# Low parts of twelve weight slabs computed by GpSimd instead of VectorE in a two-block transformer kernel

## The reference

```python
h = h + swa_sink_mixer(hn, ...)      # ends in: return o.reshape(B, S, ATTN_WIDTH) @ w_o + b_o
h = h + swiglu(rms_norm(h, ffn_norm[layer]), ffn_w_gu[layer], ffn_w_down[layer])
h = h + nsa_mixer(hn, ...)           # ends in: return o.reshape(B, S, ATTN_WIDTH) @ w_o
```

## Time and profile before

| what | us |
| --- | --- |
| median of 3 runs | 960.89 (960.56 to 962.05) |
| profiled execution, whole | 961.82 |
| its span, first to last instruction | 960.0 |
| PE busy | 938.5 (98%) |
| DVE busy | 736.5 (77%) |
| ACT busy | 545.1 (57%) |
| POOL busy | 102.3 (11%) |
| line 1777, 291 low parts on DVE | 353.7 |
| line 1218, 291 high parts on ACT | 295.9 |

### The profile page before, as it was taken

How to read it: one execution, slowest core, us unless ns; L and a number is a source line. 1 busy time by engine, 2 the same in 40 slices (tenths; PEclk the granted TensorE clock), 3 DMA queues, 4 the chain that set the end, 5 groups by cost and what they waited for, 6 DMA issues and landing times.

```text
span 960.0 us, 16452 instructions
## 1 busy us (share of the span) xinstructions
PE 938.5 (98%) x6364; PEld 842.7 (88%) x6364; DVE 736.5 (77%) x1531; ACT 545.1 (57%) x1061; POOL 102.3 (11%) x134
## 2 busy tenths in 40 slices
PE   7989999999999999999999999999999999999997
PEld 7989899988888889889888888899877988888887
DVE  6889855697777675966998888768898589888871
ACT  6667653566555465776644444558687564444452
POOL 3110002300000050003110101210000110100120
PEclk8999999999999999999999999999999999999999
DMA  8977235496454464316945645557311346445621
GB/s 284 239 193 218 88 133 176 152 259 227 158 214 175 175 220 143 121 46 198 272 159 214 220 160 191 203 173 258 113 46 45 136 173 219 177 148 201 220 88 44
DMA packets 25983, 165.12 MB, mean 172 GB/s; under 512 B 3320, under 2 KB 3704, under 8 KB 7472
## 3 DMA queue, kind: packets, MB, share of 16 engines
q1 hardware_dynamic: 23504, 156.09, 46.7%
q0 software_dynamic: 2400, 7.97, 4.4%
HBM read 161.03 MB, written 3.01 MB: 171 GB/s over the span
## 4 chain that ended last, share of the span: by engine, by line
PE 85%; DVE 5%; ACT 4%; DMA 4%; issue 1%; SPq 0%; POOL 0%; DVEq 0%
PE banks L591 22%; PE banks L911 13%; PE banks L594 11%; PE banks L915 8%; PE banks L565 4%; PE banks L569 4%; PE banks L573 4%; DMA scratch<-VR 3%; PE banks L614 3%; PE banks L616 2%; PE banks L618 2%; ACT PN L1462 1%; PE banks L840 1%; PE banks L576 1%; PE banks L577 1%
## 5 line engine op out<-in xcount | busy, mean ns | idle before, releaser
L1777 DVE TENSOR_TENSOR lo<-stage,hi 128x1024 fp32r<-128x1024 f32 x291 | 353.7, 1230 | 19.9 <-ACT hi L1218 18.2
L1218 ACT ACTIVATE hi<-stage 128x1024 fp32r<-128x1024 f32 x291 | 295.9, 1043 | 28.0 <-DMA stage<-in_stream 13.9
L591 PE MATMUL banks<-HT,hi 128*128 128x512 f32 x920 | 232.2, 394 | 0.0
L591 PEld LDWEIGHTS banks<-HT,hi 128*128 128x128 f32 x920 | 165.1, 188 | 33.7
L594 PEld LDWEIGHTS banks<-HT,lo 128*128 128x128 f32 x920 | 125.4, 189 | 9.7
L594 PE MATMUL banks<-HT,lo 128*128 128x256 f32 x920 | 128.0, 282 | 0.0
L2538 POOL TENSOR_TENSOR SQ<-SQ 128x256 f32<-128x256 f32 x40 | 43.4, 1091 | 422.9 <-ACT SQ L1236 421.9
L2276 DVE TENSOR_REDUCE U<-banks 128x256 f32<-128x512 f32 x73 | 50.3, 690 | 29.6 <-PE banks L594 29.2
L911 PE MATMUL banks<-HC,hi 128*128 128x512 f32 x196 | 70.5, 398 | 0.0
L565 PE MATMUL banks<-HT,hi 128*128 128x256 f32 (+3 forms) x348 | 56.3, 297 | 9.7 <-ACT HT L1228 4.9
L915 PE MATMUL banks<-HC,lo 128*128 128x256 f32 x224 | 63.0, 281 | 0.0
(11 more groups left out here) (348 smaller groups left out, 1785.8 us busy)
## 6 DMA issues: line engine op xcount, KB each, us to landing
stage<-in_stream SPq DMA_DIRECT2D x144, 1024.0 KB, 4.9
BT<-scratch POOLq DMA_DIRECT2D x8, 256.0 KB, 15.9
BT<-scratch POOLq DMA_DIRECT2D x4, 512.0 KB, 17.4
stage<-in_stream SPq DMA_DIRECT2D x3, 512.0 KB, 9.7
scratch<-VR POOLq DMA_DIRECT2D x2, 768.0 KB, 21.3
XT<-in_xt SPq DMA_DIRECT2D x4, 256.0 KB, 6.5
B<-scratch POOLq DMA_DIRECT2D x4, 256.0 KB, 6.4
out<-ROWS SPq DMA_DIRECT2D x4, 256.0 KB, 2.5
```

The source lines that it names most:

```text
L591: e.matmul(out[:, 0:512], hi[:, j % HI_SLOTS, 128 * k:128 * k + 128], HT[:, :, k, :], start=k == 0, stop=False)
L1218: e.activation(hi[:, j % HI_SLOTS, 0:w], stage[:, j // 2 % ST_PAIRS, j % 2, 0:w], ACT.Copy).then_inc(*up("hi", ("hi", j, 0)))
L1777: e.tensor_tensor(lo[x], stage[x], f32(hi[:, j % HI_SLOTS, 0:sched[j][2]]), ALU.subtract).then_inc(*up("lo", ("lo", j, 0)))
```

## The change

VectorE leaves out the low parts of slabs 2 to 7 of `swa_o` and of `nsa_o`, twelve in all. GpSimd does the same subtraction from the same operands, each after the high part of its slab, and counts up a semaphore of its own, `lo_pool`. In its list the first six stand behind the sum of squares of the swa layer, the other six behind the copies into `BC`. TensorE waits for the low part of a slab as before, by key. Nothing else changes.

```diff
+    "sums", "pool_step", "branch", "silu", "lo_pool",
...
+    pool_lows = {name: [slab[name, i] for i in range(2, 8)] for name in ("swa_o", "nsa_o")}
...
-        slabs = Splits(sched, lambda j: None, low_split)
+        others = set(pool_lows["swa_o"] + pool_lows["nsa_o"])
+        slabs = Splits(sched, lambda j: None, lambda j: None if j in others else low_split(j))
...
     def gpsimd(e):
         q = Queue(e)
 
+        def low_splits(name):
+
+            for j in pool_lows[name]:
+                q.wait_ge(*at("hi", j, 0))
+                e.tensor_tensor(lo[:, j // 2 % ST_PAIRS, j % 2], stage[:, j // 2 % ST_PAIRS, j % 2], f32(hi[:, j % HI_SLOTS]), ALU.subtract).then_inc(*up("lo_pool", ("lo", j, 0)))
...
         sum_squares("swa", both=True)
+        low_splits("swa_o")
         sum_squares("mlp2")
...
         e.tensor_copy(BC[:, :, 16:23], BT[:, :, 159:256:16]).then_inc(*up("pool_step", ("bc",)))
+        low_splits("nsa_o")
         sum_squares("mlp3")
```

More of the change, by code:

```diff
@@ L170 @@
     "lo", "low", "sums_dve", "x", "root_dve", "z", "top", "probabilities", "key_dve", "query_dve", "step",
-    "sums", "pool_step", "branch", "silu",
+    "sums", "pool_step", "branch", "silu", "lo_pool",
     "w0", "w1", "w2", "w3", "w4", "w5", "wone2", "wfirst0", "wfirst1", "x0", "x1", "x2", "x3", "columns", "masks",
```

## The result

| what | before | after |
| --- | --- | --- |
| median of 5 runs each, us | 962.05 (960.56 to 962.40) | 974.17 (972.24 to 975.21) |
| ratio after to before | | 1.0131 (95% interval 1.0115 to 1.0147) |
| profiled execution, whole | 961.8 | 974.2 |
| its span | 960.0 | 972.4 |

The change makes the kernel 12.1 us slower (by the interval of the ratio 11.1 to 14.1). The forecast was 972.3 us, with 962.0 to 979.5 as its range and 0.84 on slower. The total came out as forecast, but not by the terms of the forecast's sum: the blocked port cost less than forecast, and a clock that fell, which no step of the prediction had, made up for it.

What follows compares the result with a forecast made beforehand. TensorE was taken to bound both attentions, in the third waiting for a ring through ScalarE and VectorE. Port costs 8.9 + 2.5 = 11.4 us on 961.8 gave 973.2, less 0.9 for the median 972.3 us; range 962.0 to 979.5.

Steps and rivals of the forecast that it cites:

- third attention, port: Third attention: GpSimd's subtractions block VectorE's small two-SBUF lines in six steps, 2.4 + 5 x 1.3 = 8.9 us.
- second attention, port: Second attention: GpSimd's subtractions may hold up VectorE's tensor_scalars and so TensorE; taken at 2.5 us.
- relief of VectorE: Both attentions: removing 14.6 us of low parts from VectorE gains nothing, as they lie off the path TensorE waits for.
- the ring through ScalarE and VectorE: Third attention: a cycle of steps through both engines, 7.69 us from one line 1706 on, that sets TensorE's waits.
- Hold of 2.4 us: Both attentions: each 128x1024 GpSimd subtraction takes 2.4 us and excludes VectorE's two-SBUF instructions for its whole length.
- First slab 2.4: Third attention, first moved slab: GpSimd gets the port first and line 2496 waits, 2.4 us.
- Five slabs at 1.3 each: Third attention, other five moved slabs: VectorE's line 2496 goes first, then line 2451 comes 1.3 us late each time.
- Second attention 2.5 between 0 and 3.6: Second attention: 0 if tensor_scalars don't wait for the port, up to 3.6 us if they do; 2.5 taken.
- (1): Rival, both attentions: exclusion not felt, as GpSimd fits in a 1.07 us gap or 64-element instructions slip past; 960.7 us, chance 0.12.
- (2): Rival, both attentions: GpSimd wins the port each time, 6 x 2.4 + 3.6 = 18 us more, 978.9 us; chance 0.19.
- (3): Rival: the hold is shorter (1.22 to 2 us) or tensor_scalars don't wait; 963 to 969.8 us, chance 0.19.
- (4): Rival, both attentions: low parts are on TensorE's path and its waits go, 4.0 us less, 956.9 us; chance 0.04.

Runs made afterwards that it cites:

- e10: The change, with one ScalarE high part in step 5 of the second attention put behind the scale of the query tile: 972.11 us, ratio 1.0112.
- e3: The kernel before without the twelve low parts, computed by nobody; TensorE multiplies the high part again in their place: 960.67 us, ratio 0.9988.
- e5: The change, but GpSimd subtracts only the first 256 of 1024 columns of each slab and VectorE the rest, after it: 963.86 us, ratio 1.0033.
- e4: The change, but each GpSimd subtraction also waits until VectorE's small lines that need the port are over: 961.33 us, ratio 0.9999.
- e7: The change, but GpSimd copies each of the twelve slabs (one operand) instead of subtracting, so low parts are wrong: 961.41 us, ratio 1.0003.
- e9: e4 with one ScalarE high part in step 5 of the second attention put behind the scale of the query tile: 960.92 us, ratio 0.9985.
- e6: The change, but GpSimd subtracts only the first 512 of 1024 columns of each slab and VectorE the rest, after it: 965.62 us, ratio 1.0052.
- e1: The change with only the second attention's six low parts (swa_o) on GpSimd, those of nsa_o back on VectorE: 964.83 us, ratio 1.0030.

## Why the prediction was right, and which of its steps were not

The difference of 12.4 us between the profiled executions, in terms of the prediction's sum:

| term | forecast | measured | shown by |
| --- | --- | --- | --- |
| third attention, port | 8.9 | 7.1 | rings of e10 |
| second attention, port | 2.5 | 2.2 | the change's steps: 0.03 + 0.66 + 0.44 and 1.04 at ZR; no run forces it apart from the clock |
| relief of VectorE | 0 | 0.7 at best, not taken by the change | e3 |
| TensorE at half clock | not in the sum | 1.5 + 2.1 | second attention: 4.60 against 3.08 us for the same work; third: rings 4 and 5 against e10 |
| rest of the kernel | 0 | -0.5 | scatter ahead of the second attention |

- **What bounds the kernel.** Right: the ring through ScalarE and VectorE in the third attention. The ring table shows it, and e3 shows that a gain ahead of it is given back (0.2 us gained and lost again in the next step).
- **Relief costs and gives nothing.** Right in the third attention. In the second it gives 0.65 us at ZR (e3): the ZR path of VectorE and ScalarE does have a low part in it. It is small beside the rest.
- **Hold of 2.4 us.** Right: 2.34 to 2.39 us alone and 2.5 to 2.6 where it waits for line 2499 or 1853. This was extrapolated from 0.59 us for 256 elements behind the lock; four times that is 2.36. The Trainium skill (GPSIMD Engine Reference, "3. Performance versus the Vector engine") gave 2.4 as well; the trace agrees with its 2.6 cycles an element for two inputs: 0.73 us for 256 elements in e5 and 2.37 for 1024 make 2.1 ns an element, by the page's 1.2 GHz an estimate of 2.6 cycles.
- **First slab 2.4.** GpSimd goes first there, as forecast, but the instruction that it overtook, by 0.09 us, was the tensor_scalar of line 2493, ahead of line 2499, and it cost 2.1 us. The prediction had line 2496 (now 2499) wait there, and counted tensor_scalars in the second attention alone.
- **Five slabs at 1.3 each.** This is the term that was too large: 6.5 forecast, 5.0 in e10, where the clock stays up in these rings or costs nothing. In the change they are 0.7, 1.05, nothing, 1.1 and 1.05. The 0.7 is that of a step that also scales a query tile ahead of line 2454, by which the gap is 1.39 us and not 1.07; the prediction took one step as the model of all. VectorE wins the port, as taken, and line 2454 is late, as taken. But GpSimd had already started 0.1 us before line 2499 took the port, so its own start is not paid again behind the lock: from the end of line 2499 (715.37) to GpSimd's (717.61) are 2.24 us, and line 2454 at 716.42 is 1.05 us longer, since its own start is covered by the wait too (it ends 0.08 us after GpSimd). The fourth slab meets nothing in the change: behind the fall of the clock line 2454 comes only after GpSimd has ended (727.8 against 728.05), where in e10 it is blocked by 1.1.
- **Second attention 2.5 between 0 and 3.6.** The open question, whether tensor_scalars from SBUF to SBUF wait, is answered: the pair of line 2163 takes 1.90 us instead of 0.55. This is what the Trainium skill states (SBUF — State Buffer, "SBUF: two separate sides", with Advanced Engine Details and Errata, "VectorE Performance Modes"): the trace agrees. What the blocked pairs cost came out lower than the 3.6 us that the prediction worked out for this case: 2.2, and the 3.7 of the whole only with the clock. The path to TensorE was right too, over ZR, where the waits are seen.
- **The clock.** No step of the prediction asked what TensorE's idle time does to its clock. In the change it stands at half for 6.8 us in the third attention and 3.4 in the second, and 3.6 of the 12.4 us are lost to that. In the third attention this is a difference between two kernels that differ in the second attention only, so it is well supported; that the idle time causes the fall is a reading of the traces, not something an experiment forced. For it: each fall in the two attentions stands behind a wait of 1.5 us or more, and the kernels with the small losses, e3, e4 and e7 to e9, have 1.00 in both. Against idle time alone: behind waits of 3.0 and 2.8 us in the change and of 2.3 us in e10 the clock stayed up.
- **The rivals.** (1) is right that short holds are free: up to 1.14 us behind the end of line 2502 in e6 (2499 of the change), a little over the 1.07 that the prediction gave. The hold simply is 2.4, and its other reason, that a 64-element instruction slips past, is wrong (1.27 instead of 0.22). (2) happens for one slab of six, by the 0.1 us between the two starts. (3) is wrong on both counts. (4) is wrong: with no low parts at all the gain is 0.7 us, not 4.0.

So the total was right to 0.2% while 2.1 us of overestimate and 3.6 us of a missing term cancelled in part. The sign, the place and the mechanism stand; that the total came this close was luck.

What stays open: what decides whether the clock falls. With the same wait for ZR of 2.1 us it fell in e1, e5 and the change and not in e6, and e10's third attention was spared in its fourth ring while that of the change was not. As the executions of e6 differ by up to 3.6 us and in their mean clock, one profile of a kernel shows one case of several, and the 3.6 us of the clock hold for the profiled execution alone.

## What to carry to other kernels

An engine that has nothing to do is not a free engine: look at which of the neighbour's instructions need the port that it takes, and whether one of them, however small, lies in a ring. Here 0.2-us instructions in the ring turned twelve hidden subtractions into 9.3 us, 12.1 with the clock, and a wait that put the same twelve beside VectorE's reads of PSUM made them free. Idle time added to TensorE should be costed with the clock that may fall behind it, here four tenths on top in the profiled execution.

## What the runs showed of the hardware that was not expected

- A tensor_scalar of 128x258 from SBUF to SBUF waits for GpSimd's instruction to end (1.90 us for a pair, against 0.55), and so does a 64-element instruction with two SBUF operands (1.27 against 0.22). Instructions of VectorE with an operand in PSUM don't (0.41 and 0.42 beside GpSimd, as alone), nor does a reduction of 128x64 with its single operand in SBUF (0.22 at 716.09, line 2451, as alone).
- A copy of 128x1024 by GpSimd takes 1.04 us and a subtraction 2.37. The copy takes the port as well: it blocked a tensor_scalar for 0.78 us.
- The granted clock of TensorE fell to the lower level after idle times of 2.1 and 2.3 us, in a kernel whose TensorE is busy for 97% of its span, and not after 3.0 and 2.8 us in the same execution. At the lower level a product of 16 matmuls took 2.95 us instead of 1.63. Executions of one kernel (e6) had a mean clock of 0.993 to 0.989 and took 964.5 to 968.2 us.
